# Encoder block on one core: last stage closed by tiles with column sums, two of its normalizations spread over two chunks, and TensorE's order in attention grouped by map

## The chip, the cores and the metric

The kernel is one program on one core of a Trainium2 chip. The metric is the device time of that core in microseconds, the median of the runs of one kernel. TensorE multiplies matrices into PSUM, VectorE and ScalarE work on elements of PSUM and SBUF, GpSimd on SBUF alone, and SP (SyncE) issues most of the DMAs. Each engine works through its own instructions in their order in the program; between engines only semaphores order the work.

## What is computed

One encoder layer over 2048 tokens of width 1024, in float32:

```python
n    = rmsnorm(x, norm1_g)
proj = n @ w_in                       # q, k, v (4 heads), u
p    = softmax(q_c k_c^T * scale - slope * |i - j|)   # two maps c = 0, 1 a head
att  = (p_0 - lam * p_1) @ v          # then rmsnorm over the head
ssm  = glu(bi_s5(u))
h    = x + [att ; ssm] @ w_out
h    = h + relu(rmsnorm(h, norm2_g) @ w_mlp1)**2 @ w_mlp2
y    = rmsnorm(h, final_g)
```

## The kernel before, in words

Four stages follow each other: projection, attention (`phase_attention`), the SSM (`phase_ssm`) and the last stage (`phase_mlp`), which holds w_out, the MLP and the final normalization.

**Attention** walks over 64 blocks n: four heads of sixteen blocks of 128 queries, each against all 2048 keys. A block has two softmax maps (c = 0, 1); each map's scores come in two halves of 1024 keys, so that `scores(n, hf)` runs for hf = 0 to 3, with c = hf // 2. One call is four float32r matmuls of 512 columns (L1060 and L1061: the key's high and low part). There is one score buffer for each half, so `scores(n, hf)` waits until VectorE has taken the half two calls before it. VectorE (`add_bias`, L970) adds the distance bias to a half and keeps the running maximum. ScalarE (L892) takes the exponential of a whole map in place, in the tile `e`, with a sum. VectorE's `combine(n, 2)` (L996) then makes p_0 - lam * p_1 in `e`. TensorE transposes that in four groups of four (`turn(n, j)`, L1073), through two PSUM buffers. ScalarE copies each group to SBUF (`copy_turned`, L904), and TensorE multiplies it with v (`values(n, j)`, L1087: four key tiles, two instructions each). ScalarE squares and copies the result (`copy_result`). VectorE's order for block n is: halves 0 and 1 of block n, small steps, `combine(n - 1, 2)`, halves 2 and 3 of block n. ScalarE's is: high part of the next queries, copies 2 and 3 of block n-2, exponential of map 0, (a part of the next head's keys), result of block n-3, copies 0 and 1 of block n-1, exponential of map 1. TensorE's order is written out by hand and stands in the diff.

**The SSM stage** takes part with one semaphore only: `edges_ready` counts small memsets of GpSimd, `const_step` its constants.

**The last stage** runs 18 chunks k: two of w_out (MIX, one for each half of the tokens), then for each half of the tokens four UP chunks (w_mlp1) and four DOWN chunks (w_mlp2). A chunk is a Strassen-like product in seven steps i. Each step has four tiles d of twelve matmuls (L2274 to L2276: high by high, high by low, low by high, 512 columns), alternating between two sets of four PSUM banks. Ahead of each step ScalarE makes the high parts of both operands (L1981, L1993) and VectorE the low parts (L2114, L2125 or L2123), and VectorE also forms the sums of operands. After a step VectorE adds the bank to the result `res` (`leave`, L2183); in UP chunks ScalarE takes part. After chunks 0, 1, 9 and 17 the residual is whole (`whole(k)`, an event), and it is normalized over its 1024 features. ScalarE squares each tile of `res` (L2047), GpSimd adds the squares up in `sums` (L1955), TensorE sums over the partitions with a matrix of ones (`statistics`, L2282), ScalarE takes the root of 512 columns and VectorE their reciprocal (`invert`, L2188). For events 0 to 2 the tiles are then reloaded from `h_s` into the two halves of `hb`, multiplied by gain and reciprocal (`normalize`, L2196) and stored, in steps 1 to 4 of the next chunk: sixteen tiles of 128x512, four a step. Only the result of event 0 is needed by the chunk behind it (chunk 2); event 1's is first read in chunk 10, and event 2's is output.

After chunk 17, the last, the order is: last `leave` (128x2048), the two statistics, the last squares and sums, two reciprocals of 512 columns, sixteen products of 128x512 in `res` with a DMA each.

## Time and profile before

| | us |
|---|---|
| median of 3 runs | 2733.12 (2729.7 to 2736.56) |
| profiled execution | 2727.37 |
| its span | 2725.6 |
| TensorE matmuls busy | 2563.4 (94%) |
| TensorE weight loads busy | 2151.4 (79%) |
| VectorE busy | 2102.7 (77%) |
| ScalarE busy | 1407.4 (52%) |
| GpSimd busy | 329.9 (12%) |
| mean granted clock of TensorE | 0.974 of full speed |

The busy time of an engine is a sum over the whole span, with stages that have different limits. The chain of work that ended last gives 42% of the span to TensorE by name and hardly anything to the others; its largest lines are L2274 to L2276, the matmuls of the last stage, with 14% each. Matmuls overlap, so a duration of 0.39 us does not mean that one starts every 0.39 us; the distance of starts tells that. In a timeline row, "x8" merges eight instructions: the first number is the start of the first, the second the time until the end of the last.

### The profile page before, as it was taken

The page shows a single profiled execution, that of the slowest core. Times are in us where ns is not written, and L with a number is a line of the kernel's source. Part 1 is how long each engine was busy: PE and PEld are TensorE (multiplying, and loading weights), DVE is VectorE, ACT ScalarE, POOL GpSimd, SP SyncE. Part 2 cuts the span into 40 slices and gives each one's busy share as a digit, 9 for nine tenths or more (in the row PEclk, how much of TensorE's full clock was granted, in tenths as well). Part 3 has the DMA queues.
Part 4 walks back from the last instruction along what each step waited for, and adds up shares of the span by engine and source line. Part 5 has one row for each costly group of instructions (what it writes and reads, how often), then busy time and mean ns, then how long its engine had stood idle before and what let it go on. Part 6 is the DMA issues. An engine that isn't in the chain of part 4 may idle for free. (4 is left out here: it accounts for less than half of the span.)

```text
span 2725.6 us, 32534 instructions
## 1 busy us (share of the span) xinstructions
PE 2563.4 (94%) x12768; PEld 2151.4 (79%) x12768; DVE 2102.7 (77%) x2078; ACT 1407.4 (52%) x1721; POOL 329.9 (12%) x219
## 2 busy tenths in 40 slices
PE   7998988999999988986988999999999999999996
PEld 5887766999999976875867788888887788888885
DVE  5866638999999967775898876677888876678886
ACT  3266616878787762223344565643434556543332
POOL 6310001101010002320334000000014000000002
PEclk9999998999999999998999999999999999999998
DMA  5356534020212018967555744452233744452211
GB/s 179 114 185 228 209 100 101 24 68 24 69 37 63 24 38 248 253 196 269 187 217 194 283 170 182 174 200 109 93 110 138 297 181 170 170 201 93 104 66 62
DMA packets 162648, 397.17 MB, mean 146 GB/s; under 512 B 29504, under 2 KB 87104, under 8 KB 134720
## 3 DMA queue, kind: packets, MB, share of 16 engines
q1 hardware_dynamic: 145792, 319.07, 35.0%
q10 hardware_dynamic: 16704, 76.03, 7.0%
q8 instruction: 101, 1.65, 0.3%
q14 instruction: 51, 0.42, 0.1%
HBM read 270.79 MB, written 122.16 MB: 144 GB/s over the span
## 5 line engine op out<-in xcount | busy, mean ns | idle before, releaser
L2274 PE MATMUL ml_bank<-ml_b_split,ml_w_split 128*128 128x512 f32 x2016 | 791.3, 393 | 33.7 <-issue 27.0
L2275 PE MATMUL ml_bank<-ml_b_split,ml_w_split 128*128 128x512 f32 x2016 | 788.1, 391 | 0.0
L2276 PE MATMUL ml_bank<-ml_b_split,ml_w_split 128*128 128x512 f32 x2016 | 787.7, 391 | 0.0
L2274 PEld LDWEIGHTS ml_bank<-ml_b_split,ml_w_split 128*128 128x128 f32 x2016 | 381.0, 189 | 120.4 <-issue 41.0
L2275 PEld LDWEIGHTS ml_bank<-ml_b_split,ml_w_split 128*128 128x128 f32 x2016 | 380.8, 189 | 79.9 <-issue 1.0
L2276 PEld LDWEIGHTS ml_bank<-ml_b_split,ml_w_split 128*128 128x128 f32 x2016 | 380.7, 189 | 79.8
L1981 ACT ACTIVATE ml_b_split<-ml_q 128x2048 fp32r<-128x2048 f32 x108 | 206.9, 1915 | 456.6 <-PE ml_bank L2276 439.5
L2114 DVE TENSOR_TENSOR ml_b_split<-ml_q,ml_b_split 128x2048 fp32r<-128x2048 f32 x108 | 247.0, 2287 | 160.9 <-ACT ml_b_split L1981 160.9
L1955 POOL TENSOR_TENSOR ml_sums<-ml_sums,ml_square 128x512 f32<-128x512 f32 x56 | 145.8, 2604 | 1302.6 <-ACT ml_square L2047 1296.6
L892 ACT ACTIVATE at_e<-at_e,at_neg_top 128x2048 f32<-128x2048 f32 x128 | 256.5, 2004 | 38.4 <-DVE at_neg_top L977 38.3
L2183 DVE TENSOR_TENSOR ml_res<-ml_bank,ml_res 128x2048 f32<-128x2048 f32 x76 | 173.8, 2287 | 130.6 <-PE ml_bank L2276 130.6
L1087 PEld LDWEIGHTS at_pv<-at_v,at_a_t 128*128 128x128 f32 x2048 | 257.5, 191 | 16.4
L1087 PE MATMUL at_pv<-at_v,at_a_t 128*128 128x128 f32 x2048 | 258.9, 275 | 0.0
L1060 PE MATMUL at_score<-at_k_hi,at_q_hl 128*128 128x512 f32 x512 | 224.6, 439 | 20.9 <-DVE at_q_hl L954 18.0
L1993 ACT ACTIVATE ml_w_split<-ml_r 128x2048 fp32r<-128x2048 f32 x108 | 205.2, 1900 | 6.9 <-DVE ml_r L2164 6.9
L2125 DVE TENSOR_TENSOR ml_w_split<-ml_r,ml_w_split 128x2048 fp32r<-128x2048 f32 x90 | 207.8, 2308 | 0.0
L1061 PE MATMUL at_score<-at_k_lo,at_q_hl 128*128 128x512 f32 x512 | 203.3, 397 | 0.0
L970 DVE CUSTOM_DVE_ANT_0 at_e<-at_score,at_bias,at_top 128x1024 f32<-128x1024 f32 x128 | 164.4, 1284 | 41.5 <-PE at_score L1061 28.0
L904 ACT ACTIVATE at_a_t<-at_turned 128x512 f32<-128x512 f32 x256 | 137.7, 588 | 97.2 <-PE at_turned L1073 97.2
L697 PE MATMUL pj_acc<-pj_x_hi,pj_w_hi 128*128 128x512 f32 x384 | 153.2, 399 | 11.6 <-DVE pj_x_lo L595 11.6
L970 DVE CUSTOM_DVE_ANT_0 at_e<-at_score,at_bias 128x1024 f32<-128x1024 f32 x128 | 156.3, 1221 | 3.5 <-DVE at_bias L1024 0.6
L996 DVE SCALAR_TENSOR_TENSOR at_e<-at_e,at_coef 128x2048 f32<-128x2048 f32 x64 | 150.5, 2352 | 2.1
(199 smaller groups left out, 3686.4 us busy)
## 6 DMA issues: line engine op xcount, KB each, us to landing
ml_r<-in_w_stream SPq DMA_DIRECT2D x72, 1024.0 KB, 5.5
ml_q<-hn_s SPq DMA_DIRECT2D x32, 1024.0 KB, 5.0
act_s<-ml_res ACTq DMA_DIRECT2D x32, 1024.0 KB, 4.7
ml_q<-act_s SPq DMA_DIRECT2D x32, 1024.0 KB, 4.8
tab_s<-pj_tab ACTq DMA_DIRECT2D x32, 512.0 KB, 2.9
pj_x_raw<-in_x_t SPq DMA_DIRECT2D x14, 1024.0 KB, 8.1
h_s<-ml_res ACTq DMA_DIRECT2D x12, 1024.0 KB, 3.9
ml_hb<-h_s SPq DMA_DIRECT2D x24, 512.0 KB, 4.4
```

Of the source, the lines that this page charges most:

```text
L892: act.activation(e[:, n % 2, c], e[:, n % 2, c], ACT.Exp, bias=neg_top[:, n % 2, c:c + 1], scale=SCALE, accum_out=esum[:, n % 2, c:c + 1]) ...
L970: dve.tensor_tensor_reduce(out=e[:, s % 2, c, half * HALF:(half + 1) * HALF], in0=score[:, half], in1=bias[:, at:at + HALF], scale=1.0, sc ...
L1060: pe.matmul(out, q_hl[:, s % 2, c], k_hi[:, h % 2, c, cols], start=True, stop=False)
L1061: last = pe.matmul(out, q_hl[:, s % 2, c], k_lo[:, h % 2, c, cols], start=False, stop=True)
L1087: last = pe.matmul(pv[:, n % 2, 0:P], a_t[:, n % 2, kt], v[:, h % 2, kt], start=(kt == 0), stop=(kt == NQ - 1))
L1981: act.activation(b_split[:, g % 2, 0], raw_b(k, i)[:], ACT.Copy).then_inc(b_hi_ready, 1)
L1993: act.activation(w_split[:, g % 2, 0], raw_w(k, i)[:], ACT.Copy, scale=-1.0 if i == 6 else 1.0)\
L2114: dve.tensor_tensor(b_split[:, g % 2, 1], raw_b(k, i)[:], b_split[:, g % 2, 0].bitcast(F32), ALU.subtract)\
L2125: dve.tensor_tensor(lo, raw_w(k, i)[:], hi, ALU.subtract).then_inc(w_lo_ready, 1)
L2274: pe.matmul(out, w_hi[:, w], b_hi[:, b], start=fresh and kt == 0, stop=False, skip_group_check=True)
L2275: pe.matmul(out, w_hi[:, w], b_lo[:, b], start=False, stop=False, skip_group_check=True)
L2276: last = pe.matmul(out, w_lo[:, w], b_hi[:, b], start=False, stop=kt == 3, skip_group_check=True)
```

## The change

Three things are changed. In attention TensorE issues both halves of a map right after each other, and all four transposes of block n-1 in block n. In the last stage the normalizations of events 1 and 2 take two chunks each, two tiles a step (`event_half`; the tiles of steps 1 to 4 of the first chunk, then of the second). And the close after chunk 17 is made anew. The last block leaves PSUM tile by tile. The sums over partitions are made with the data as the stationary operand and one column of ones (`column_sums`), so that root and reciprocal work on 128x4. A product with an identity spreads the reciprocals over the partitions again (`spread_out`). ScalarE applies the gains (`apply_gain`), and VectorE multiplies eight pairs of tiles straight from PSUM, each with one DMA of 512 KB. The first column sums stand ahead of the last tile of matmuls. The square of the last tile goes into the column sums without GpSimd. In the SSM stage `edges_ready` becomes part of `const_step`.

```diff
             for n in range(NS):
                 scores(n, 0)
-                turn(n - 2, 2)
-                turn(n - 2, 3)
                 scores(n, 1)
                 values(n - 2, 0)
                 values(n - 2, 1)
+                values(n - 2, 2)
                 scores(n, 2)
-                values(n - 2, 2)
                 scores(n, 3)
-                values(n - 2, 3)
                 turn(n - 1, 0)
                 turn(n - 1, 1)
-            turn(NS - 2, 2)
-            turn(NS - 2, 3)
+                values(n - 2, 3)
+                turn(n - 1, 2)
+                turn(n - 1, 3)
...
+    def event_half(k):
+
+        if k > 2 and whole(k - 2):
+            return EVENT[k - 2], 4
+        if k > 1 and whole(k - 1):
+            return EVENT[k - 1], 0
+        return None
...
-                    if event is not None:
+                    if event_half(k) is not None:
+                        at, first = event_half(k)
+                        if i == 0:
+                            load_hb(at, first)
+                            load_hb(at, first + 1)
+                        if i in (2, 3):
+                            store_hb(at, first + i - 2)
+                            load_hb(at, first + i)
+                        if i in (4, 5):
+                            store_hb(at, first + i - 2)
+                    elif event is not None:
...
-            for n in range(16):
-                reg, d = TILES[n // 4], n % 4
+            for n in range(8):
+                reg, d = TILES[n // 2], 2 * (n % 2)
                 j, t = J_T[reg]
                 sp.wait_ge(norm_ready, 16 * last + n + 1)
-                sp.dma_start(y_t[(j * 4 + d) * P:(j * 4 + d + 1) * P, tokens(1, t)], res[reg][:, d]).then_inc(hb_stored[0], 16)
+                sp.dma_start(y_rows[j, :, d:d + 2, tokens(1, t)], res[reg][:, d:d + 2]).then_inc(hb_stored[0], 16)
...
+            pool.memset(ident[:], 0.0).then_inc(ident_zeroed, 1)
+            pool.wait_ge(ident_zeroed, 1)
+            pool.affine_select(out=ident[:], in_=ident[:], compare_op=ALU.not_equal, fill=1.0, base=0,
+                               pattern=[[-1, P]], channel_multiplier=1).then_inc(consts_ready, 1)
...
             e = EVENT[NCH - 1]
-            rms(e, 0, banks[(NSTEP - 2) % 2][:, 3])
-            squares(NCH - 1, C21)
-            rms(e, 1, banks[(NSTEP - 2) % 2][:, 2])
+            for d in range(2):
+                square_last(d)
+            root_columns(e, 0)
+            for d in range(2, 4):
+                square_last(d)
+            root_columns(e, 1)
+            for d in range(4):
+                apply_gain(C21, d)
...
-                    if i in (1, 2, 3, 4):
+                    if i in (1, 2, 3, 4) and event_half(k) is None:
...
+                if event_half(k) is not None and i in (1, 2, 3, 4):
+                    at, first = event_half(k)
+                    group = first + i - 1
+                    dve.wait_ge(hb_loaded[group % 2], 16 * (4 * at + group // 2 + 1))
+                    for n in (2 * group, 2 * group + 1):
+                        normalize(at, n, hb[:, group % 2, n % 2], KD if at >= 2 else 0)
-            leave(NCH - 1, STEPS - 1)
             e = EVENT[NCH - 1]
-            for n in range(16):
-                if n == 0:
-                    invert(e, 0)
-                if n == 8:
-                    invert(e, 1)
-                if n % 4 == 0:
-                    dve.wait_ge(squared, squared_by(e, TILES[n // 4], 3))
-                normalize(e, n, res[TILES[n // 4]][:, n % 4], KD)
+            for d in range(4):
+                if d == 3:
+                    invert_columns(e, 0)
+                leave_tile(NCH - 1, d)
+            for n in range(4):
+                scale_out(e, n)
+                if n == 1:
+                    invert_columns(e, 1)
+            for n in range(4, 8):
+                scale_out(e, n)
...
+            def column_sums(e, n):
+
+                pe.wait_ge(added, 14 * e + (10, 13)[n])
+                if n:
+                    pe.wait_ge(squared, 16 * (e + 1))
+                totals = [sums[:, 1 - n]] + [hb[:, 0, 0]] * n
+                for c in range(TB // P):
+                    for i, total in enumerate(totals):
+                        last = pe.matmul(columns(n)[:, c:c + 1], total[:, c * P:(c + 1) * P], ones[:, 0:1],
+                                         start=(i == 0), stop=(i == len(totals) - 1))
+                last.then_inc(stat_done, 1)
...
                     slot(k, i, d)
+                    if g == NSTEP - 1 and d == 2:
+                        evacuated(pe, k, 5)
+                        column_sums(EVENT[k], 0)
...
-            statistics(e, 0, banks[(NSTEP - 2) % 2][:, 3])
-            statistics(e, 1, banks[(NSTEP - 2) % 2][:, 2])
+            spread_out(EVENT[NCH - 1], 0)
+            column_sums(EVENT[NCH - 1], 1)
+            spread_out(EVENT[NCH - 1], 1)
```

## Rows read from the trace of the kernel before

**Rows 1.** Stretches: us; busy us (instructions) of each engine; granted clock; DMA share, GB/s.
```profile
416.00:1011.00 595.00, 584.78 (x4096) 532.15 (x4096) 533.74 (x971) 456.91 (x798) 37.92 (x28) 0.99 0.18 45
1011.00:1261.00 250.00, 212.34 (x1024) 173.36 (x1024) 172.53 (x276) 70.01 (x144) 59.08 (x57) 0.93 0.78 222
1261.00:2701.00 1440.00, 1397.45 (x6069) 1145.95 (x6070) 1121.85 (x525) 691.21 (x471) 140.78 (x55) 0.99 0.44 167
```

**Rows 2.** Timeline of TensorE, attention: start us, us, engine line op [idle before <-releaser].
```profile
607.48 0.48 PE L1060 MATMUL at_score<-at_k_hi,at_q_hl 128*128 128x512 f32 x1
...
608.25 0.40 PE L1061 MATMUL at_score<-at_k_lo,at_q_hl 128*128 128x512 f32 x1
...
610.05 0.40 PE L1061 MATMUL at_score<-at_k_lo,at_q_hl 128*128 128x512 f32 x1
...
614.82 1.05 PE L1087 MATMUL at_pv<-at_v,at_a_t 128*128 128x128 f32 x8
615.71 1.04 PE L1073 MATMUL at_turned<-at_ident,at_e 128*128 128x128 f32 x8
616.50 0.47 PE L1060 MATMUL at_score<-at_k_hi,at_q_hl 128*128 128x512 f32 x1
```

**Rows 3.** Timeline of VectorE, the same block.
```profile
610.63 1.28 DVE L970 CUSTOM_DVE_ANT_0 at_e<-at_score,at_bias,at_top 128x1024 f32<-128x1024 f32 x1 [0.48 <-PE at_score L1061]
...
612.74 2.35 DVE L996 SCALAR_TENSOR_TENSOR at_e<-at_e,at_coef 128x2048 f32<-128x2048 f32 x1
615.01 1.22 DVE L970 CUSTOM_DVE_ANT_0 at_e<-at_score,at_bias 128x1024 f32<-128x1024 f32 x1
...
616.41 1.28 DVE L970 CUSTOM_DVE_ANT_0 at_e<-at_score,at_bias,at_top 128x1024 f32<-128x1024 f32 x1 [0.17 <-issue]
```

**Rows 4.** Timeline of VectorE, the last combination of attention.
```profile
1001.14 2.35 DVE L996 SCALAR_TENSOR_TENSOR at_e<-at_e,at_coef 128x2048 f32<-128x2048 f32 x1
```

**Rows 5.** Timeline of TensorE behind it.
```profile
1003.54 1.09 PE L1073 MATMUL at_turned<-at_ident,at_e 128*128 128x128 f32 x8 [2.46 <-DVE at_e L996]
1004.47 1.95 PE L1087 MATMUL at_pv<-at_v,at_a_t 128*128 128x128 f32 x16
```

**Rows 6.** Timeline of ScalarE, the block of rows 2 and 3.
```profile
612.17 2.00 ACT L892 ACTIVATE at_e<-at_e,at_neg_top 128x2048 f32<-128x2048 f32 x1
...
616.41 1.09 ACT L904 ACTIVATE at_a_t<-at_turned 128x512 f32<-128x512 f32 x2 [1.20 <-PE at_turned L1073]
```

**Rows 7.** Timeline of TensorE, last stage: first matmuls of two late steps.
```profile
1524.99 0.76 PE L2274 MATMUL ml_bank<-ml_b_split,ml_w_split 128*128 128x512 f32 x1 [4.24 <-issue]
...
2156.63 0.47 PE L2274 MATMUL ml_bank<-ml_b_split,ml_w_split 128*128 128x512 f32 x1 [1.99 <-issue]
```

**Rows 8.** Timeline of VectorE, chunk 10 (three rows) and chunk 11.
```profile
2112.07 2.74 DVE L2196 SCALAR_TENSOR_TENSOR ml_hb<-ml_hb,ml_gain,ml_rinv 128x512 f32<-128x512 f32 x4
...
2116.93 2.29 DVE L2125 TENSOR_TENSOR ml_w_split<-ml_s_first,ml_w_split 128x2048 fp32r<-128x2048 f32 x1
...
2137.56 1.41 DVE L2196 SCALAR_TENSOR_TENSOR ml_hb<-ml_hb,ml_gain,ml_rinv 128x512 f32<-128x512 f32 x2 [1.06 <-DMA ml_hb<-h_s]
...
2191.64 2.29 DVE L2114 TENSOR_TENSOR ml_b_split<-ml_t_first,ml_b_split 128x2048 fp32r<-128x2048 f32 x1 [1.50 <-ACT ml_b_split L1981]
```

**Rows 9.** Timeline of VectorE, the close.
```profile
2703.26 3.34 DVE L2188 RECIPROCAL ml_rinv<-ml_rinv 128x512 f32<-128x512 f32 x1
...
2717.49 5.39 DVE L2196 SCALAR_TENSOR_TENSOR ml_res<-ml_res,ml_gain,ml_rinv 128x512 f32<-128x512 f32 x8
```

**Rows 10.** Timeline of GpSimd, the close: fourth sum of C12's squares.
```profile
2697.80 1.28 POOL L1955 TENSOR_TENSOR ml_sums<-ml_sums,ml_square 128x512 f32<-128x512 f32 x1 [0.43 <-POOL ml_sums L1955]
```

**Rows 11.** DMA issues of the close: count, KB each, median us to landing.
```profile
y_t<-ml_res SPq DMA_DIRECT2D x16, 256.0 KB, 2.2
```

**Rows 12.** Group of a GpSimd select; TensorE's first matmul of the last stage.
```profile
L863 POOL TENSOR_SCALAR_AFFINE_SELECT at_ident<-at_ident 128x128 f32<-128x128 f32 x1 | 4.5, 4450 | 0.0
...
1275.70 0.76 PE L2274 MATMUL ml_bank<-ml_b_split,ml_w_split 128*128 128x512 f32 x1 [6.37 <-DVE ml_w_split L2125]
```

More of the change, by code:

```diff
@@ L1949, in add_squares @@
                 for d in range(4):
-                    if at < 2 and d == 0:
+                    if at < 2 and d == 0 or k == NCH - 1 and reg == C21 and d == 3:
                         continue
@@ L1963, in _, with columns, spread @@
                         add_squares(k, reg)
+        spare = banks[(NSTEP - 2) % 2]
+        def columns(n):
+            return spare[:, 2 * n, 0:TB // P]
+        def spread(n):
+            return spare[:, 2 * n + 1]
         def raw_b(k, i):
@@ L2064, in store_res, with square_last, root_columns, apply_gain @@
                 act.dma_start(dst.rearrange("p (d t) -> p d t", d=4), res[reg][:]).then_inc(res_stored[reg], 16)
+            def square_last(d):
+                e = EVENT[NCH - 1]
+                act.wait_ge(dve_left, COUNT[NCH - 1, 6] + d)
+                n = 14 * e + 10 + d
+                if d < 3:
+                    act.wait_ge(added, n - 1)
+                    dst = square[:, n % 2]
+                else:
+                    for b in range(2):
+                        act.wait_ge(hb_stored[b], 16 * 4 * e)
+                    dst = hb[:, 0, 0]
+                act.activation(dst, res[C21][:, d], ACT.Square).then_inc(squared, 1)
+            def root_columns(e, n):
+                act.wait_ge(stat_done, 2 * e + (1, 3)[n])
+                act.activation(rms_c[:, n], columns(n), ACT.Sqrt, bias=eps_c[:], scale=1.0 / D).then_inc(rms_ready, 1)
+            def apply_gain(reg, d):
+                act.wait_ge(squared, squared_by(EVENT[NCH - 1], reg, d))
+                at = KD + J_T[reg][0] * 4 + d
+                act.activation(res[reg][:, d], res[reg][:, d], ACT.Copy, scale=gain[:, at:at + 1]).then_inc(in_place_ready, 1)
             split_high_b(0)
             split_high_w(0)
-            act.wait_ge(consts_ready, 19)
+            act.wait_ge(consts_ready, 20)
             for g in range(NSTEP):
@@ L2096, in _ @@
                 if whole(k):
-                    if i == 2:
-                        squares(k, C11)
-                    if i == 5:
-                        squares(k, C22)
-                    if i == 6:
-                        squares(k, C12)
-            e = EVENT[NCH - 1]
-            rms(e, 0, banks[(NSTEP - 2) % 2][:, 3])
-            squares(NCH - 1, C21)
-            rms(e, 1, banks[(NSTEP - 2) % 2][:, 2])
+                    if i in (2, 5, 6):
+                        reg = {2: C11, 5: C22, 6: C12}[i]
+                        squares(k, reg)
+                        if not following:
+                            for d in range(4):
+                                apply_gain(reg, d)
+            e = EVENT[NCH - 1]
+            for d in range(2):
[6 more added lines that the diff above has]
+                apply_gain(C21, d)
         @block.vector
@@ L2183, in leave, with leave_tile, invert_columns, scale_out @@
                 dve.tensor_tensor(flat(res[reg]), flat(bank(k, i)), flat(res[reg]), ALU.add).then_inc(dve_left, 1)
+            def leave_tile(k, d):
+                dve.wait_ge(slot_done, 4 * (k * STEPS + 6) + d + 1)
+                evacuated(dve, k - 1, 6)
+                dve.tensor_tensor(res[C21][:, d], bank(k, 6)[:, d], res[C21][:, d], ALU.add).then_inc(dve_left, 1)
+            def invert_columns(e, n):
+                dve.wait_ge(rms_ready, 2 * e + n + 1)
+                dve.reciprocal(rms_c[:, n], rms_c[:, n]).then_inc(rinv_ready, 1)
+            def scale_out(e, n):
+                reg, half = TILES[n // 2], n % 2
+                if n % 4 == 0:
+                    dve.wait_ge(stat_done, 2 * e + 2 + n // 4 + 1)
+                dve.wait_ge(in_place_ready, 2 * UP_NO[NCH - 1] + 4 * SQUARES.index(reg) + 2 * half + 2)
+                rows = res[reg][:, 2 * half:2 * half + 2]
+                dve.tensor_tensor(rows, rows, spread(n // 4).unsqueeze(1).to_broadcast([P, 2, TB]), ALU.mult)\
+                    .then_inc(norm_ready, 1)
             def invert(e, n):
@@ L2242, in _ @@
                             normalize(event, n, hb[:, n // 2 % 2, n % 2], KD if kind(k - 1) == DOWN else 0)
-            leave(NCH - 1, STEPS - 1)
-            e = EVENT[NCH - 1]
-            for n in range(16):
-                if n == 0:
-                    invert(e, 0)
-                if n == 8:
-                    invert(e, 1)
-                if n % 4 == 0:
-                    dve.wait_ge(squared, squared_by(e, TILES[n // 4], 3))
-                normalize(e, n, res[TILES[n // 4]][:, n % 4], KD)
+                if event_half(k) is not None and i in (1, 2, 3, 4):
[4 more added lines that the diff above has]
+                        normalize(at, n, hb[:, group % 2, n % 2], KD if at >= 2 else 0)
+            e = EVENT[NCH - 1]
+            for d in range(4):
+                if d == 3:
[7 more added lines that the diff above has]
+                scale_out(e, n)
         @block.tensor
@@ L2282, in statistics, with spread_out @@
                 pe.matmul(out, ones[:], sums[:, 1 - n], start=True, stop=True).then_inc(stat_done, 1)
-            pe.wait_ge(consts_ready, 19)
+            def column_sums(e, n):
[8 more added lines that the diff above has]
+                last.then_inc(stat_done, 1)
+            def spread_out(e, n):
+                pe.wait_ge(rinv_ready, 2 * e + n + 1)
+                for c in range(TB // P):
+                    last = pe.matmul(spread(n)[:, c * P:(c + 1) * P], rms_c[:, n, c:c + 1].to_broadcast([P, P]), ident[:],
+                                     start=(c == 0), stop=(c == TB // P - 1), skip_group_check=True)
+                last.then_inc(stat_done, 1)
+            pe.wait_ge(consts_ready, 20)
             for d in range(4):
```

27 lines of the change are left out of this document (14 added, 13 removed).

## The prediction

> **What bounds the kernel now.** I read the stages first, from the table of stretches [rows 1]. In attention TensorE is busy 584.78 of 595 us, in the last stage (w_out and the MLP) 1397.45 of 1440 us; both hang on TensorE, and only what makes TensorE wait there is worth anything. Second, the timeline of one block of attention (one head, 128 queries, two maps). From the first score matmul of one block at 607.48 to that of the next at 616.50 is 9.02 us, and no row between carries idle time [rows 2]: 16 score matmuls some 0.23 apart and 48 of 128 columns some 0.111 apart (0.89 for eight, 614.82 to 615.71). VectorE has 0.48 us in which it waits for scores [rows 3]. So an order of TensorE can gain next to nothing here. The question is whether it can lose, and for that the waits between the engines have to be followed round the loop. Third, the last stage: TensorE idles where VectorE comes late with a split, at 1524.99 (4.24 us) and 2156.63 (1.99 us; a step ahead at 2143.48 it is much the same) [rows 7]. Fourth, the close: from about 2701, where VectorE adds the last block ahead of the reciprocal at 2703.26, to the end at 2725.6 us TensorE has nothing but small work, and VectorE has two reciprocals of 3.34 us and sixteen products [rows 9].
>
> **Attention, the largest term.** VectorE's and ScalarE's orders are not touched. VectorE does, for block n: bias and maximum of the first map's halves (L970, twice), small steps, the combination of block n-1 (L996), then the other two halves. TensorE now issues both score calls of the first map, three quarters of values, the other two score calls, and only then turn(n-1, 0). Turn(n-1, 0) waits for the combination of n-1, the combination stands on VectorE behind the halves of scores(n, 0) and (n, 1), and all that TensorE has left after the turns stands behind them. That is a loop; its length from rows:
> - scores(n, 0) from its first start to its end: 607.48 to 608.25 + 0.40, 1.17 us [rows 2];
> - VectorE sees it: scores(n, 1) ended at 610.05 + 0.40 = 610.45 and L970 began at 610.63, 0.18 us [rows 2, 3];
> - first half to second: 615.01 to 616.41, 1.40 us; scores(n, 1) are ready by then, since they follow 0.91 us behind (1.17 + 0.91 + 0.18 = 2.26 against 1.35 + 1.40 = 2.75);
> - second half to combination: 610.63 to 612.74, 2.11 us; the combination itself 2.35 us [rows 3];
> - VectorE to turn: the last combination ends at 1001.14 + 2.35 = 1003.49, the turn starts at 1003.54, 0.05 us [rows 4, 5];
> - two turns after an idle TensorE: 1003.54 to 1004.47, 0.93 us [rows 5]; values(n-2, 3), 0.89 us (614.82 to 615.71); the last two turns up to the next block's scores, 0.79 us (615.71 to 616.50) [rows 2].
>
> Sum: 1.17 + 0.18 + 1.40 + 2.11 + 2.35 + 0.05 + 0.93 + 0.89 + 0.79 = 9.87 us, against 9.02 now: 0.85 us more for each block. In the order of before the same combination ends at 612.74 + 2.35 = 615.09 and the turn comes at 615.71, with 0.6 us to spare, and behind it only 0.79 us of turns stand before the next scores; the other two turns come after scores(n, 0), where VectorE works on those scores. That cover goes: 1.8 us of turns and values move from behind the scores to ahead of them.
>
> Queued behind the waiting turn: turn 1, values(n-2, 3), turns 2 and 3, scores(n+1). Who waits for that: VectorE for the next scores, at no further cost, as it is the same loop. ScalarE: its exponential starts 1.54 us behind the second half (610.63 to 612.17) and takes 2.00; a copy starts 0.70 behind its turn (615.71 to 616.41) and two take 1.09 [rows 6]. Copy 0 would end about 1.3 us behind turn 0, while turn 2 comes 1.82 behind it; copy 1 ends at 1.8, turn 3 comes at 2.27. So ScalarE does not lengthen the loop; with 0.4 us to spare that is its weakest point. Half the groups of scores, and so half of the changes between 512 and 128 columns, give at most 0.05 us a block (9.02 against 16 x 0.227 + 48 x 0.111 = 8.96), and it vanishes in a wait.
>
> 61 blocks pay 0.85 us (52). The second block pays about 1: its turns 2 and 3 now wait for the copies. At the three changes of head VectorE's halving of the bias makes it late today, some 3 us together, and would hide in its new idle time of about 1.2 us. Attention: **+50 us**. Bounds: 0.75 to 0.95 a block, 44 to 56, as the two reactions are each one reading of about 0.1 us.
>
> **Last stage, chunks 2 and 3, 10 and 11.** Two normalized tiles a step in place of four, eight of sixteen one chunk later. One costs 0.66 us of VectorE (four in 2.74 at 2112.07), and four stand ahead of the split that step 3 waits for (ready 2116.93 + 2.29 = 2119.22) [rows 7, 8]. Two fewer bring step 3 on by 1.3 us at most, in two chunks: the statistics matmul just before it caps that, I take 1.2 each, 2.4. Ahead of the split for step 5 VectorE first waits for a reload of `hb` and then multiplies, until 2137.56 + 1.41 = 2138.97 [rows 8]. With two tiles, loaded a step earlier, the wait goes, and so do the idle 4.24 us in chunk 2 with about 1 us of half-rate matmuls behind it (0.76 us for the first instead of 0.47), and about 2 us twice in chunk 10 [rows 7]. Sum 2.4 + 4.2 + 1 + 4 = 11.6, with the pipeline's refilling **-12 us**. In chunks 3 and 11 the two tiles of a step take 1.4 us, and VectorE idles 1.50 us ahead of the split at 2191.64 [rows 8]: no cost; without that cover it would be 1.4 us a step. Chunk 1 keeps its four a step, so its waits, the late load of chunk 2 and the wait for GpSimd's sums at its start stay. SP's queue gets its stores and loads a step later in the new chunks, behind loads of weights that wait for steps already past. Bounds -6 (the reload only moves) to -15.
>
> **The close.** Added ahead of the end: TensorE waits after the third tile of its last step for GpSimd's sum, which ended at 2697.80 + 1.28 = 2699.08 [rows 10], 0.9 us behind that tile, then the first column sums, 8 instructions I take at 0.111 us, as the 128-column ones of attention (0.06 to 0.25): the last tile ends near 2703.0 in place of 2701.0. VectorE adds it alone, 2.29/4 and a fixed part, 0.65 us, to 2703.7. The reciprocal of 512 columns (3.34 us, twice [rows 9]) becomes one of 4, some 0.2. The gains are ScalarE's, in gaps it has. Eight products of 1024 elements at 1.2 us (the 1024-element L970 takes 1.22 [rows 3]) stand in place of sixteen at 0.66. VectorE: two products to 2706.4; square of the last tile 0.63, second column sums 1.8, root: 2706.9; reciprocal; six products to 2714.1. Last store 512 KB against 256 KB that took 2.2 us [rows 11]: 3.2, and the end near 2717.6 in place of 2725.6: **-8 us**. Bounds -4 (column sums at 0.25, products slower from PSUM) to -11.
>
> **Edits at nothing.** The identity on GpSimd (a select as in attention, 4.45 us [rows 12]) delays TensorE's clearing matmuls, behind which it idles 6.37 us before 1275.70 [rows 12]. Without that cover up to 4.5 us. The merged semaphore of the SSM stage waits for the same memsets.
>
> **How the numbers follow.** 50 - 12 - 8 = +30 us. The profiled run took 2727.37 us (span 2725.6), so it becomes 2757; it lies 5.7 us under the median of the runs, 2733.12, which becomes **2763 us**.
>
> **Rivals.**
> - Faster: attention does not pay. The point is where the combination ends: if 6.3 us behind scores(n, 0) instead of 7.2, turn 0 finds it ready. For it: VectorE no longer waits its 0.48 us. Against it: the loop above starts at the scores of the same block, so that VectorE can't run ahead. It gives 2733 - 12 - 8 - 1 = 2712 us. Chance 0.10. Half of the 0.85 hidden: 2737, 0.05.
> - The waits of chunks 2 and 10 move to another step, as the reload of `hb` is slow (VectorE waits for it ahead of the pair at 2137.56 [rows 8]): 2775 us. Chance 0.10.
> - The clock. TensorE would idle some 0.9 us in every block. The SSM stage, where it is busy 212.34 of 250 us, has a granted clock of 0.93 against 0.99 in attention [rows 1]. Half-rate for 14% of a block would add some 0.5 us to each, 30 us: 2793. Against it: behind the idle 1.99 us at 2156.63 the matmuls are at full rate, behind 4.24 us they are not [rows 7]. All of it at 1.2 GHz would be 2.5 us of turns and values and 0.9 of scores more a block, 2970 us. Chance of the two 0.05. The Trainium skill ("TensorE: Matmul & The Clock Gate", section "A second HAM failure mode: psum-queue depth-cycling") tells that frequent short idles between groups of matmuls can make the clock swing between its levels; it speaks for this rival, and no row of attention shows such idles yet.
> - The forecast: 0.70.
>
> The range is 2742 to 2782: the forecast with its bounds (2763 and 44 to 56, 6 to 15, 4 to 11 combined, and the 3 us by which the runs differ) and the second rival. A measurement tells 0.3%, 8 us, from no change: faster 0.11, within 0.05, slower 0.84.
>
> **What would show it.** Attention: blocks 9.87 us apart, idle time of about 0.9 us before turn 0, ended by L996, 60 times; VectorE idle 1.2 us a block for scores. Chunks 2 and 10 without idle time before steps 5 and 6; chunk 11 without any. Reciprocals of 0.2 us, an end 14 to 16 us behind the last product matmul. Wrong, if blocks stay 9.0 apart, if turn 2 waits for ScalarE, or if score matmuls start 0.43 apart.

## The result and the profile after

The changed kernel takes 2772.7 us (median of four runs, 2772.25 to 2772.91) against 2733.01 us for the kernel before (2729.7 to 2736.56): a ratio of 1.0143, 95% interval 1.0128 to 1.0158. It is 1.4% slower. The profiled execution took 2772.9 us with a span of 2771.1 us.

| | before | after |
|---|---|---|
| median, us | 2733.01 | 2772.7 |
| span of the profiled execution | 2725.6 | 2771.1 |
| attention (first score matmul to last values matmul) | 594.2 | 652.6 |
| SSM stage (from there to the first product of the last stage) | 264.8 | 267.5 |
| last stage (first to last product matmul) | 1425.3 | 1416.6 |
| close (from there to the end) | 24.6 | 17.7 |

The spans differ by 45.5 us: +58.4 in attention, +2.7 in the SSM stage, -8.7 in the last stage and -6.9 in the close. By the medians it is 39.7: the profiled execution of before, 2727.37 us, lay 5.6 us under its median, that of the changed kernel on it.

First the stretches, as in [rows 1] with the borders moved to the new stages: us; busy us (instructions) of TensorE, its weight loads, VectorE, ScalarE, GpSimd; granted clock; DMA share, GB/s.

```profile
416.00:1070.00 654.00, 594.65 (x4096) 527.07 (x4096) 533.49 (x971) 463.22 (x800) 38.14 (x28) 0.99 0.16 41
1070.00:1336.00 266.00, 219.34 (x1032) 175.49 (x1032) 175.26 (x278) 73.65 (x144) 61.32 (x62) 0.92 0.80 227
1336.00:2753.00 1417.00, 1391.21 (x6067) 1145.22 (x6068) 1124.15 (x528) 696.17 (x485) 141.47 (x55) 0.99 0.44 166
```

The same 4096 matmuls of attention keep TensorE busy for 594.65 us, 9.87 more than before, in a stretch 59 us longer, and VectorE's busy time is unchanged at 533. The granted clock is 0.99 as before. So 49 of the 59 us are idle time. The other 9.87 are no added work: the last matmul ahead of a wait counts as busy to its end (622.80 + 0.39 in the rows below), where the next would otherwise start 0.23 us behind it, 0.16 us in each block. The table of waits of TensorE in attention (engine, tile, line, who ended the wait: us in total, times, longest) has the idle time in one row; in the kernel before, the same row has 6.2 us in 5 waits:

```profile
PE at_turned L1073 <- DVE at_e L996: 52.3, 63, 2.4
```

One block on TensorE (start, us, engine, line, operation, tiles, shape, count, [idle before <- who ended it]); in [rows 2] no row of the block had idle time:

```profile
616.59 0.48 PE L1060 MATMUL at_score<-at_k_hi,at_q_hl 128*128 128x512 f32 x1
...
618.52 2.84 PE L1087 MATMUL at_pv<-at_v,at_a_t 128*128 128x128 f32 x24
...
622.80 0.39 PE L1061 MATMUL at_score<-at_k_lo,at_q_hl 128*128 128x512 f32 x1
623.98 1.09 PE L1073 MATMUL at_turned<-at_ident,at_e 128*128 128x128 f32 x8 [0.79 <-DVE at_e L996]
624.91 1.06 PE L1087 MATMUL at_pv<-at_v,at_a_t 128*128 128x128 f32 x8
625.80 1.04 PE L1073 MATMUL at_turned<-at_ident,at_e 128*128 128x128 f32 x8
626.59 0.48 PE L1060 MATMUL at_score<-at_k_hi,at_q_hl 128*128 128x512 f32 x1
```

From the first score matmul of one block to that of the next: 616.59 to 626.59, 10.00 us, against 9.02. The order on the queue is the new one, the turn starts 0.79 us late, and its releaser is the combination, L996. VectorE in the same block:

```profile
617.94 1.23 DVE L970 CUSTOM_DVE_ANT_0 at_e<-at_score,at_bias 128x1024 f32<-128x1024 f32 x1 [1.22 <-PE at_score L1061]
...
619.46 1.28 DVE L970 CUSTOM_DVE_ANT_0 at_e<-at_score,at_bias,at_top 128x1024 f32<-128x1024 f32 x1 [0.29 <-DVE at_top L970]
...
621.57 2.35 DVE L996 SCALAR_TENSOR_TENSOR at_e<-at_e,at_coef 128x2048 f32<-128x2048 f32 x1
623.84 1.22 DVE L970 CUSTOM_DVE_ANT_0 at_e<-at_score,at_bias 128x1024 f32<-128x1024 f32 x1
...
625.24 1.28 DVE L970 CUSTOM_DVE_ANT_0 at_e<-at_score,at_bias,at_top 128x1024 f32<-128x1024 f32 x1 [0.17 <-issue]
```

Both engines now idle in each block, TensorE for VectorE's combination and VectorE 1.22 us for TensorE's scores; in [rows 3] VectorE waited 0.48 us. That is the mark of a chain of dependencies that goes round through both, with the block's time as its length; that it is this chain was tried in e5, e6 and e9.

The last stage, waits of TensorE. The first row here is of the kernel before (its L2274 is L2363 now), the other two are of after:

```profile
PE ml_bank L2274 <- issue: 27.0, 10, 7.1
```

```profile
PE ml_bank L2363 <- issue: 16.7, 7, 7.0
PE ml_bank L2371 <- POOL ml_sums L1973: 6.8, 3, 3.6
```

A late step is one whose first matmul comes with idle time ahead of it. Three of the ten are gone (4.24 us in chunk 2, 2.04 and 1.99 in chunk 10) and two more shrink from some 1.55 to 0.23 us, while the one at the start of chunk 2 grew by 0.9: 10.3 us less idle time in all. The close on VectorE, which answers to [rows 9]:

```profile
2750.93 0.18 DVE L2255 RECIPROCAL ml_rms_c<-ml_rms_c 128x4 f32<-128x4 f32 x1 [1.56 <-ACT ml_rms_c L2113]
2753.48 0.69 DVE L2250 TENSOR_TENSOR ml_res<-ml_bank,ml_res 128x512 f32<-128x512 f32 x1 [2.38 <-PE ml_bank L2365]
...
2756.95 2.35 DVE L2264 TENSOR_TENSOR ml_res<-ml_res,ml_bank 128x1024 f32<-128x1024 f32 x2 [2.78 <-PE ml_bank L2381]
...
2759.31 6.87 DVE L2264 TENSOR_TENSOR ml_res<-ml_res,ml_bank 128x1024 f32<-128x1024 f32 x6
```

The two reciprocals of 3.34 us take 0.18 and 0.17 us, and the eight products take 1.15 to 1.18 us each. But the first product starts after 2.78 us of idle time, and VectorE is done at 2766.2, 4.9 us before the end. The DMA of that stretch (GB/s in 40 slices of 2750 to 2772; then issues: count, KB each, median us to landing):

```profile
GB/s 0 0 0 0 0 0 0 0 0 0 0 0 0 0 0 0 160 395 361 395 365 372 376 387 372 380 380 372 384 384 372 376 369 391 384 391 261 0 0 0
...
y_t<-ml_res SPq DMA_DIRECT2D x8, 512.0 KB, 3.7
```

From the first store on, the queue moves 361 to 395 GB/s without a gap until they are written: the stores, not the products, set the end. (e7 below tests it.)

### The profile page after: what moved, and what is told of

It is laid out like the page before. It is cut to its first block and busy times, and to the rows that moved or that the text cites. A ratio compares the mean times of both kernels' runs of the same rounds, so it can differ in the third digit from the quotient of the medians.

```text
span 2771.1 us, 32612 instructions
## 1 busy us (share of the span) xinstructions
PE 2577.2 (93%) x12804; PEld 2152.3 (78%) x12804; DVE 2096.8 (76%) x2073; ACT 1421.9 (51%) x1737; POOL 328.3 (12%) x220
## 5 line engine op out<-in xcount | busy, mean ns | idle before, releaser
L2363 PE MATMUL ml_bank<-ml_b_split,ml_w_split 128*128 128x512 f32 x2016 | 792.3, 393 | 23.3 <-issue 16.7
L2363 PEld LDWEIGHTS ml_bank<-ml_b_split,ml_w_split 128*128 128x128 f32 x2016 | 381.1, 189 | 109.0 <-issue 29.4
L1087 PE MATMUL at_pv<-at_v,at_a_t 128*128 128x128 f32 x2048 | 249.2, 275 | 0.0
L1087 PEld LDWEIGHTS at_pv<-at_v,at_a_t 128*128 128x128 f32 x2048 | 243.4, 192 | 4.8
L1060 PE MATMUL at_score<-at_k_hi,at_q_hl 128*128 128x512 f32 x512 | 214.1, 418 | 20.4 <-DVE at_q_hl L954 18.1
L1073 PE MATMUL at_turned<-at_ident,at_e 128*128 128x128 f32 x1024 | 136.4, 276 | 55.7 <-DVE at_e L996 55.4
L1073 PEld LDWEIGHTS at_turned<-at_ident,at_e 128*128 128x128 f32 x1024 | 112.7, 141 | 82.8 <-DVE at_e L996 82.2
```

The source lines that it names most:

```text
L1060: pe.matmul(out, q_hl[:, s % 2, c], k_hi[:, h % 2, c, cols], start=True, stop=False)
L1073: last = pe.transpose(turned[:, j % 2, i * P:(i + 1) * P], e[:, n % 2, 0, kt * P:(kt + 1) * P], ident[:])
L1087: last = pe.matmul(pv[:, n % 2, 0:P], a_t[:, n % 2, kt], v[:, h % 2, kt], start=(kt == 0), stop=(kt == NQ - 1))
L2363: pe.matmul(out, w_hi[:, w], b_hi[:, b], start=fresh and kt == 0, stop=False, skip_group_check=True)
```

## The experiments

All were run beside the kernel before. "Stage times" are those of the table above, read from each kernel's trace. Line numbers in the rows are those of the kernel they come from.

### The change in two halves

**e1, attention alone:** the kernel before with only TensorE's new order.

```
             for n in range(NS):
                 scores(n, 0)
-                turn(n - 2, 2)
-                turn(n - 2, 3)
                 scores(n, 1)
                 values(n - 2, 0)
                 values(n - 2, 1)
-                scores(n, 2)
                 values(n - 2, 2)
+                scores(n, 2)
                 scores(n, 3)
-                values(n - 2, 3)
                 turn(n - 1, 0)
                 turn(n - 1, 1)
+                values(n - 2, 3)
+                turn(n - 1, 2)
+                turn(n - 1, 3)
-            turn(NS - 2, 2)
-            turn(NS - 2, 3)
```

> The kernel before with TensorE's new order in attention and nothing else. If the loop scores - combination - turns - next scores sets the distance of blocks: 10.00 us a block as in the changed kernel, attention 58 us longer, in all 2733 + 58 = 2791 us, and the SSM stage behind it as long as before. If part of those 58 us comes with the other edits: under 2780 us. If the 2.7 us that the SSM stage grew by come from the later start of that stage, it is 2.7 us longer here too; if they come from the merged semaphore, it is not.

Measured 2790.42 us, ratio 1.0213 (1.0198 to 1.0227), attention 656.3 us. Its waits of TensorE in attention:

```profile
PE at_turned L1073 <- DVE at_e L996: 51.9, 63, 2.3
```

**e2, the last stage alone:** the changed kernel with attention's old order (the edit of e1 undone). **e3, the close alone:** e2 without the normalization over two chunks:

```
     def event_half(k):
-        if k > 2 and whole(k - 2):
-            return EVENT[k - 2], 4
-        if k > 1 and whole(k - 1):
-            return EVENT[k - 1], 0
         return None
```

> The changed kernel with TensorE's order in attention as before: new close, normalizations over two chunks, merged semaphore. If the parts add up: 2772.7 - 58 = 2715 us, blocks 9.02 us apart, chunks 2 and 10 without idle time ahead of steps 5 and 6, the close 17.7 us behind the last matmul. If the merged semaphore costs the 2.7 us seen in the SSM stage, they are here as well (264.8 us from the end of attention to the first product matmul of the last stage without, 267.5 with). If the last stage gains only because attention ends later: nearer to 2725 us.

> As the kernel with the last stage alone, but the normalizations of events 1 and 2 in one chunk each again, so that only the close (and the merged semaphore) differs from before. If the two traces are read rightly, chunks 2 and 10 lose 16.8 and 10.2 us again instead of 10.8 and 4.2, and the kernel takes 12 us more than with the spread normalizations, 2727 us; the close alone is then worth 5 us. Rival: the waits of chunks 2 and 10 shrank for another reason (order of the stores and loads behind a different end of attention): both kernels the same.

Measured: e2 2713.51 us, ratio 0.9937 (0.9924 to 0.9949); e3 2727.58 us, 0.999 (0.998 to 1.0). The waits of TensorE in the last stage, first e3, then e2:

```profile
PE ml_bank L2361 <- issue: 26.5, 11, 7.0
```

```profile
PE ml_bank L2365 <- issue: 16.0, 8, 6.9
```

What follows: the attention order costs 60 us wherever it stands (e1 over before, 60.0 by the 2730.41 us that before took beside it; after over e2 59.2 by their medians, some 56 by their ratios to before, 58.6 by the attention stage of their traces), and the rest of the change is a gain of 17. Of that, spreading the normalization brings 14 us (e3 to e2), the close 3 (before to e3), at the edge of what the runs tell from nothing. In e3's trace the close is 7.0 us shorter and the last step ahead of it 2.1 us longer.

### Which loop it is

**e4, grouping by itself:** scores grouped, but the four turns of a block split over two blocks, as before.

```
                 scores(n, 0)
+                scores(n, 1)
                 turn(n - 2, 2)
                 turn(n - 2, 3)
-                scores(n, 1)
                 values(n - 2, 0)
                 values(n - 2, 1)
-                scores(n, 2)
                 values(n - 2, 2)
+                scores(n, 2)
                 scores(n, 3)
                 values(n - 2, 3)
```

> The kernel before with the score calls of a map grouped, but with the turns at their old places: two of block n-2 behind the first pair of scores, turn(n-1, 0) and (n-1, 1) last. Loop theory: the combination is ready some 7.4 us behind the block's first score, the turn comes at 8.1, nothing waits, 9.0 to 9.1 us a block, 2733 us in all (2728 to 2738). Rival, the grouping itself costs (VectorE gets its second half too early or too late, or TensorE pays for the order): near 10.0 us a block and 2790 us.

Measured 2754.94 us, ratio 1.0089 (1.0076 to 1.0102): 24.5 us slower than before and not about equal, attention 621.8 us, 9.41 us a block. The expectation was wrong. VectorE in one block, then TensorE behind it:

```profile
616.70 1.23 DVE L970 CUSTOM_DVE_ANT_0 at_e<-at_score,at_bias 128x1024 f32<-128x1024 f32 x1
...
618.81 1.28 DVE L970 CUSTOM_DVE_ANT_0 at_e<-at_score,at_bias,at_top 128x1024 f32<-128x1024 f32 x1 [0.88 <-PE at_turned L1073]
...
624.58 1.28 DVE L970 CUSTOM_DVE_ANT_0 at_e<-at_score,at_bias,at_top 128x1024 f32<-128x1024 f32 x1 [0.17 <-issue]
...
628.22 1.28 DVE L970 CUSTOM_DVE_ANT_0 at_e<-at_score,at_bias,at_top 128x1024 f32<-128x1024 f32 x1 [0.89 <-PE at_turned L1073]
```

```profile
625.93 0.50 PE L1060 MATMUL at_score<-at_k_hi,at_q_hl 128*128 128x512 f32 x1
...
626.97 1.03 PE L1073 MATMUL at_turned<-at_ident,at_e 128*128 128x128 f32 x8
```

VectorE's second half writes the buffer of `at_e` that turn(n-2, 3) reads, and waits for that turn (0.88 us idle, releaser `at_turned`). The turn now stands behind scores(n, 1), which waits until VectorE has read the last half of block n-1 (624.58 + 1.28 = 625.86, scores at 625.93). The turns end at 626.97 + 1.03 = 628.00, and the next second half starts at 628.22, 9.41 us behind the one at 618.81. So grouping alone closes a second loop: last half, scores(n, 1), turns, first map's second half. It is read from these rows; no link of this one was taken out. Moving all four turns ahead, as the change does, opens this loop and closes the one of 10.00 us. Both orders with grouped scores cost time; in the order of before neither loop binds, as TensorE has no idle time in a block [rows 2].

**e5 and e6: one link of the loop taken out at a time.** In e5 VectorE's `q_low(n + 1)` (0.42 us, L954) goes behind the combination; in e6 values(n-2, 3) go ahead of the turns.

```
                 combine(n - 1, 1)
+                combine(n - 1, 2)
                 if n + 1 < NS:
                     q_low(n + 1)
-                combine(n - 1, 2)
```

```
                 scores(n, 3)
+                values(n - 2, 3)
                 turn(n - 1, 0)
                 turn(n - 1, 1)
-                values(n - 2, 3)
                 turn(n - 1, 2)
```

> The changed kernel, but VectorE makes the low part of the next queries (0.42 us and its issue, 0.46 us) behind the combination, not ahead of it. The same work on every engine. Loop theory: that step leaves the loop between scores and turns, a block takes 10.00 - 0.46 = 9.54 us, 2772.7 - 28 = 2745 us. Rival, TensorE's idle time before the turns comes from the order of its own instructions or from its clock: 10.00 us and 2773 us, as the total work of VectorE is the same.

> The changed kernel, but values(n-2, 3) stands ahead of turn(n-1, 0) and fills the time in which TensorE waits for the combination. Loop theory: behind the turn stand only turns 1 to 3; turns 2 and 3 now wait for ScalarE's copies (1.3 and 1.8 us behind turn 0), so the next scores come 2.3 us behind turn 0 in place of 2.61: 9.7 us a block, 2754 us. If ScalarE's copies weigh more than the values: 10.0 us. If only TensorE's amount of work counted: 9.1.

Measured: e5 2746.18 us, ratio 1.0062 (1.0045 to 1.0079), 9.55 us a block; e6 2756.61 us, 1.0099 (1.0083 to 1.0115), 9.69 to 9.70 a block. TensorE's waits in attention, first e5, then e6:

```profile
PE at_turned L1073 <- DVE at_e L996: 17.5, 57, 0.9
```

```profile
PE at_turned L1073 <- ACT at_a_t L904: 17.7, 57, 0.3
PE at_turned L1073 <- DVE at_e L996: 1.6, 5, 0.5
```

The two stand 26.5 and 16.1 us under the changed kernel's 2772.7 (by the ratios to the kernel before, whose runs beside these had a median of 2728.59, it is some 22 and 12); in attention alone they are 24.8 and 16.7 us shorter. In e5 0.42 us of VectorE's work is moved, on an engine that is idle for 1.22 us of each block, and each block is 0.45 shorter: that is what a loop through that instruction does, and TensorE's amount of work or its clock would not. In e6 the wait for the combination is gone (5 instead of 63 times), as 0.89 us of values now lie in front of the turn; the block doesn't fall back to 9.02 us, because turn 2 then waits for ScalarE's copy, 0.31 us each time. That was the prediction's "weakest point": with the values moved, ScalarE is on the loop. The two edits together were not tried.

**e9, one wait of VectorE less.** `add_bias` had one wait more for map 0 than for map 1, for turns that are long done; with it the second half has three waits (turns, scores, first half), without it two. In the changed order the turns of block n-2 stand on TensorE's queue ahead of scores(n, 0), so the wait for these scores covers them.

```
                 hf = 2 * c + half
-                if c == 0:
-                    wait(dve, turned_done, 4 * (n - 2) + 2 * half + 2)
                 dve.wait_ge(scores_done, 4 * n + hf + 1)
```

> The changed kernel without VectorE's wait for the turns of block n-2 ahead of the halves of map 0. With the new order those turns stand ahead of scores(n, 0) on TensorE, for which VectorE waits anyway. The second half of map 0 starts 1.52 us behind the first, of map 1 1.40, and this wait is the difference between them. If it is the cause: 1.40 for both, 9.88 us a block, 2765 us. If not (the longer distance comes from VectorE's having been idle): 10.00 and 2773.

Measured 2767.94 us, ratio 1.0143 (1.0128 to 1.0158). That is 4.8 us under the changed kernel's median, but the kernel before took 2728.59 us beside it and 2733.01 beside the changed one, so the times don't tell the two apart; the traces do. The blocks are 9.90 us apart from the fourth on, against 10.00. VectorE:

```profile
625.60 1.22 DVE L967 CUSTOM_DVE_ANT_0 at_e<-at_score,at_bias 128x1024 f32<-128x1024 f32 x1 [1.23 <-PE at_score L1058]
...
627.00 1.28 DVE L967 CUSTOM_DVE_ANT_0 at_e<-at_score,at_bias,at_top 128x1024 f32<-128x1024 f32 x1 [0.17 <-issue]
```

First half to second is 1.40 us (625.60 to 627.00) instead of the 1.52 of the changed kernel (617.94 to 619.46), and the idle time between them 0.17 instead of 0.29. This is the predicted 1.40, and 9.90 is within 0.03 of the predicted 9.87 us. Over 60 blocks 0.10 is 6.0 us, while attention as a whole is 3.8 us shorter (648.8 against 652.6): the second and third block took 11.57 and 10.78 us in e9 (10.39 and 10.00 in the changed kernel), as they did in e1 (11.56 and 10.89), where no wait is removed. e2 and e12, which are one kernel, took 18.2 and 20.8 us for these two blocks together. So they differ from one execution to the next, whatever the edit; the cause stays open.

### The close and the small costs

**e7 and e11, the same kernel twice:** e2, in which the first half's products wait for the first column sums only. The count waited for is the last of three steps (column sums 0, spread 0, column sums 1), where the second is enough.

```
                 if n % 4 == 0:
-                    dve.wait_ge(stat_done, 2 * e + 2 + n // 4 + 1)
+                    dve.wait_ge(stat_done, 2 * e + 2 + 2 * (n // 4))
```

> The changed kernel with TensorE's attention order as before, and the first four products of the close waiting for the first spread of the reciprocals (count 2 of stat_done) and no longer for the second column sums (count 3). The first product starts some 2.5 us earlier. If the close is set by the 4.2 MB of output at 380 GB/s from the first store on: the close 2.5 us shorter, 2711 us. If by VectorE's products behind the second root: 1.9 us or less.

> The kernel with the new last stage and the earlier products once more, beside the one without them on the same chip. Output-bound close: 2.5 us less than the other, by the medians, 2710 against 2713; the close 15.1 us behind the last matmul against 17.7.

**e12:** e2 again, beside e11.

> The kernel with the new last stage and TensorE's attention order as before, once more, as the partner of the kernel with the earlier products: 0.6% faster than before, 17 us, as in its first run; 2.5 us slower than its partner.

Measured: e7 2709.77 us, ratio 0.9932 (0.9916 to 0.9947); e11 2711.38 us, 0.9928 (0.9916 to 0.994); e12 2712.59 us, 0.993 (0.9916 to 0.9943). VectorE's first products in e7:

```profile
2699.63 2.35 DVE L2266 TENSOR_TENSOR ml_res<-ml_res,ml_bank 128x1024 f32<-128x1024 f32 x2 [0.37 <-PE ml_bank L2391]
```

The close shrinks from 17.7 to 15.2 us (15.3 in e11), as the wait of 2.78 us becomes 0.37. The last store is issued 8.43 us behind the first in e7 and 8.00 in the changed kernel, as VectorE's products have a gap now; the end comes 12.89 and 12.91 us behind the first all the same. So it is the stores that set the end. The medians, however, lie only 1.2 us apart on one chip (e11 to e12), which these runs can't tell from nothing. The traces show what took part of it, in the last step of TensorE in e7:

```profile
2693.22 1.02 PE L2383 MATMUL ml_bank<-ml_ones,ml_sums 128*128 128x1 f32 x8 [0.93 <-POOL ml_sums L1975]
...
2695.12 0.43 PE L2366 MATMUL ml_bank<-ml_b_split,ml_w_split 128*128 128x512 f32 x1
...
2695.77 0.63 PE L2365 MATMUL ml_bank<-ml_b_split,ml_w_split 128*128 128x512 f32 x1
2696.20 0.63 PE L2366 MATMUL ml_bank<-ml_b_split,ml_w_split 128*128 128x512 f32 x1
```

Behind the 0.93 us wait and eight matmuls of one column each, matmuls first run at full pace and from 2695.35 on at half of it (0.43 us from 2695.77 to 2696.20 in place of 0.23; the granted clock is 1.00 from 2694.10 to 2695.35 and 0.50 from there to 2698.53), and the last step takes 14.6 us (14.5 in e11). In the changed kernel, e2, e3, e5, e6 and e12 the same step took 13.1 to 13.2 at full pace. It isn't the edit of e7 that does it: e9, whose close is that of the changed kernel, has 14.6 too. Three profiles of nine that have these column sums show it; what decides it stays open.

**e8 and e10:** the kernel before once more, and the kernel before with the SSM stage's two semaphores merged as in the change:

```
-                pool.memset(x_st[:, slot, :, edge:edge + 1], 0.0).then_inc(edges_ready, 1)
-            pool.wait_ge(const_step, 2)
+                pool.memset(x_st[:, slot, :, edge:edge + 1], 0.0).then_inc(const_step, 1)
+            pool.wait_ge(const_step, 2 + XR)
...
-            pe.wait_ge(edges_ready, XR)
+            pe.wait_ge(const_step, 2 + XR)
```

> The kernel before once more, for a second profile of it. It shows how far the stages scatter from one execution to the next: if the SSM stage (264.8 us from the last matmul of attention to the first product matmul of the last stage) comes out between 264 and 271 us here, the 2.7 us by which it was longer in the changed kernel are scatter.

> The kernel before with the merged semaphore of the SSM stage alone. If the merging costs the 2.7 us: 2733 us against 2730. If it costs nothing: the same as before, within 0.1%.

Measured: e8 2730.78 us, ratio 0.9994 (0.9984 to 1.0004); e10 2728.97 us, 0.9989 (0.9977 to 1.0001). The SSM stage took 264.6 us in both, against 264.8 in before: the merged semaphore costs nothing. The other kernels had 264.3 to 270.5 us there, the changed one 267.5. e1 and e4, whose SSM stage is that of before, had 270.3 and 268.5, so the 2.7 us need no edit; what scatters the stage was not found.

## Why the prediction was right, and where it was off

Direction, range and cause were right: +30 us predicted, +39.7 measured (2763 and 2772.7 us, in a range of 2742 to 2782). Between the two profiled executions, from which the terms were read, the miss is larger: +45.5 us against +30. Of these 15.5 us attention has 8.4, the close 3.2, the SSM stage 2.7 and the rest of the last stage 1.2. That the medians came out nearer, 9.7 us off, is luck: the profiled execution of before lay low among its runs.

**What bounds it, right.** "An order of TensorE can gain next to nothing" [rows 2], and it lost. e1 and e2 show that the whole loss is the order.

**Attention, right as a mechanism, one link mis-sized.** +50 predicted, +58.4 in the stage. Link by link in the block shown above:

| link | predicted | measured, from the rows of after |
|---|---|---|
| scores(n, 0) to first half | 1.17 + 0.18 | 616.59 to 617.94, 1.35 |
| first half to second | 1.40 | 617.94 to 619.46, **1.52** |
| second half to combination | 2.11 | 619.46 to 621.57, 2.11 |
| combination to turn | 2.35 + 0.05 | 621.57 to 623.98, 2.41 |
| turn, values, turns, next scores | 0.93 + 0.89 + 0.79 | 623.98 to 626.59, 2.61 |
| sum | 9.87 | 10.00 |

The 1.40 was read at 615.01 and 616.41, which are the halves of map 1 [rows 3]; the loop goes through those of map 0, and these have a wait more in front of them. e9 took that wait out and got 1.40 and 9.90 us a block. Over 61 blocks 0.12 is 7.3 of the 8.4 us by which attention was under-called; the bound of 0.95 a block was 0.03 short (0.98). The three changes of head took 10.45, 10.12 and 10.12 us (10.33, 9.97 and 9.97 before), so the lateness there hid in the idle time nearly as said. The second block took 10.39, about 1 us over the 9.38 of before, as said.

That ScalarE doesn't lengthen the loop was right for the change: 63 of TensorE's waits for turns name VectorE, one of 0.2 us ScalarE. In e6, where turn 2 follows turn 1 directly, ScalarE is the releaser.

**Chunks 2 and 10, right.** -12 predicted. From the first matmul of a chunk to that of the next, chunk 2 became 5.9 us shorter (92.9 to 87.0) and chunk 10 6.0 (86.3 to 80.3), and e2 is 14 us under e3 by the medians. Term by term: the step ahead of step 3 is 1.33 us shorter in each (1.2 said), the steps with the idle 4.24 us and what follows it 5.9 (5.2 said), the two in chunk 10 4.7 (4 said). The first step of chunk 2 was 1.3 us longer, which took part of that back. It took 20.1 to 20.3 us in three of the eight traces with the spreading, and 18.8 to 19.0 us in the other five and in all six without it; whether the spreading does it stays open. VectorE in chunk 10 of after, the pair and the split behind it, which answer to the third of [rows 8]:

```profile
2185.45 1.31 DVE L2278 SCALAR_TENSOR_TENSOR ml_hb<-ml_hb,ml_gain,ml_rinv 128x512 f32<-128x512 f32 x2
...
2187.58 2.29 DVE L2175 TENSOR_TENSOR ml_b_split<-ml_q,ml_b_split 128x2048 fp32r<-128x2048 f32 x1 [0.82 <-ACT ml_b_split L2011]
```

No wait for a reload stands before the pair any more (1.06 us in [rows 8]), and the split behind it waits 0.82 us for ScalarE, so VectorE is early. By the waits it is TensorE's idle time of kind "issue" that went, 10.3 us, and the rest is slower matmuls behind it. The rival in which the waits only move to another step is false. Chunk 11, where the two tiles were costed at nothing because VectorE idled 1.50 us ahead of the split:

```profile
2240.41 1.41 DVE L2278 SCALAR_TENSOR_TENSOR ml_hb<-ml_hb,ml_gain,ml_rinv 128x512 f32<-128x512 f32 x2
...
2241.99 2.29 DVE L2175 TENSOR_TENSOR ml_b_split<-ml_t_first,ml_b_split 128x2048 fp32r<-128x2048 f32 x1 [0.17 <-ACT ml_b_split L2011]
```

1.41 us of work went into that gap and 0.17 is left. The cover held, by 0.17 us.

**The close, right in sign, too large.** -8 predicted; -6.9 behind the last product and +2.1 in the last step, -4.8 together, near the small end of 4 to 11. (e3 has -2.8 by the medians.) The end lies 17.7 us behind the last product matmul, where 14 to 16 were said. The sum itself has a slip of 0.3 us: 2714.1 + 3.2 is 2717.3, not 2717.6. The cost ahead was right: 2.0 us predicted for the sums between the third and fourth tile, 2.1 measured, 0.93 of waiting and 0.9 for the column sums. Two things failed behind it. First, the two first products were taken to go out behind the first spread, while the code waits one count further, for the second column sums; the spread ended at 2754.33 and the first product began at 2756.95. TensorE in after, the spread and the sums behind it:

```profile
2753.28 1.05 PE L2389 MATMUL ml_bank<-ml_ident,ml_rms_c 128*128 128x128 f32 x8
2754.98 0.35 PE L2381 MATMUL ml_bank<-ml_ones,ml_sums 128*128 128x1 f32 x2 [0.64 <-ACT ml_hb L2108]
```

With the count corrected the close is 2.4 us shorter (e7, e11), as far as the traces go.

Second, the end was put 3.2 us behind the last store, as if the stores kept up with VectorE. They don't. From the first store of the close to the end it was 12.86 to 12.92 us in each kernel with 512 KB stores, whether the products came early or late. That is 4.19 MB at 325 GB/s, latencies at both ends included. Before, with sixteen stores of 256 KB behind slower products, it was 18.1, and the last of them ended 2.7 us ahead of the end (2717.49 + 5.39 against 2725.6): VectorE set the pace. So VectorE's part of the gain ended where DMA took over.

**Edits at nothing.** The merged semaphore is at nothing (e10). The select ahead of the clearing matmuls lay in the SSM stage, whose +2.7 us is inside the scatter of that stage (e1 and e4 have neither edit and were longer still); it was not tried alone.

**Rivals.** "Attention does not pay" (2712 us) and half of it are false: 63 waits, 52.3 us. The clock is false: the granted clock of attention is 0.99, and the scores start 0.23 us apart. The Trainium skill ("TensorE: Matmul & The Clock Gate", section "A second HAM failure mode: psum-queue depth-cycling") says that frequent short idles between groups of matmuls can make the clock go up and down; with an idle of 0.79 us in each block of 10 us this trace shows no such thing.

**The best version.** The parts that pay, with the close's count corrected and attention as before: 2709.77 and 2711.38 us in two sets of runs (e7, e11), 0.7% faster than the kernel before and by the ratios 2.1% faster than the changed one. The corrected count is seen in the traces alone: e12, without it, has the same ratio, 0.993.

## What to carry to other kernels

When an in-order queue has no idle time, a new order can still lose: write down the chain of dependencies that goes round through both engines back to itself, add it up from rows, and compare it with the time of an iteration, taking each link's time from the very instruction on the chain with all its waits. Such a chain closes where an instruction that waits has been put ahead of work that used to stand in front of it. And before shortening what feeds a final burst of stores, divide their bytes by the rate that the trace shows.

## What the hardware did that was not expected

- A semaphore wait whose condition had long been met cost VectorE 0.12 us: 1.52 us between two starts with three waits ahead of the second, 1.40 with two, on the same instruction (after and e9).
- Behind 0.93 us of idle time and 0.9 us of one-column matmuls TensorE's clock fell from 2.4 to 1.2 GHz in three profiles of nine (matmuls of 512 columns 0.43 us apart in place of 0.23), and cost 1.4 us, while an idle of 0.79 us in each block of attention left it at 0.99.
- Stores of 512 KB from one core ran at 361 to 395 GB/s, back to back.
